# A hybrid decoder layer with 32 experts: expert weights loaded in transfers of two neighbouring units

## The reference

```python
x = x + jnp.einsum('bsd,de->bse', merged, w_out[l])
x = x + _moe(_rms_norm(x, g_ffn[l], RMS_EPS), w_router[l], b_router[l], w1[l], b1[l], w2[l], b2[l])
# in _moe: 32 experts, the top 4 of each token; for the tokens xb of an expert e:
gu = xb @ w1[e] + b1[e]                      # w1[e]: 1024 x 2048
gate, up = gu[:, :D_EXPERT], gu[:, D_EXPERT:]
gate = jnp.minimum(gate, SWIGLU_LIMIT)
up = jnp.clip(up, -SWIGLU_LIMIT, SWIGLU_LIMIT)
act = (up + 1.0) * (gate * jax.nn.sigmoid(SWIGLU_ALPHA * gate))
yb = act @ w2[e] + b2[e]                     # w2[e]: 1024 x 1024
```

## Time and profile before

| | us |
|---|---|
| median of 3 runs | 1905.17 (1902.64 to 1905.51) |
| profiled execution | 1906.27 |
| its span, first to last instruction | 1904.5 |
| mean granted TensorE clock | 0.993 of full speed |
| TensorE matmul busy | 1853.2 (97%) |
| VectorE busy | 1121.7 (59%) |
| ScalarE busy | 941.0 (49%) |
| GpSimd busy | 335.9 (18%) |
| DMA moved | 511.61 MB, mean 269 GB/s |

### The profile page before, as it was taken

How to read it: one execution, slowest core, us unless ns; L and a number is a source line. 1 busy time by engine, 2 the same in 40 slices (tenths; PEclk the granted TensorE clock), 3 DMA queues, 4 the chain that set the end, 5 groups by cost and what they waited for, 6 DMA issues and landing times.

```text
span 1904.5 us, 27272 instructions
## 1 busy us (share of the span) xinstructions
PE 1853.2 (97%) x8668; PEld 1311.0 (69%) x8668; DVE 1121.7 (59%) x1364; ACT 941.0 (49%) x1310; POOL 335.9 (18%) x401
## 2 busy tenths in 40 slices
PE   7999999999999999998999999999999999999998
PEld 5888888888888888886656655566556655665563
DVE  6767768768768433356745654455545654655466
ACT  4665765765667322234544444345435543445341
POOL 0321321322321000012111121112211220122010
PEclk8999999999999999998999999999999999999999
DMA  5231231331231332356899999999999999999998
GB/s 176 78 102 44 102 102 44 102 102 48 98 124 34 100 100 99 120 202 266 359 421 421 422 421 421 421 422 421 421 421 422 421 421 422 421 421 421 422 418 340
DMA packets 88286, 511.61 MB, mean 269 GB/s; under 512 B 12820, under 2 KB 15932, under 8 KB 37944
## 3 DMA queue, kind: packets, MB, share of 16 engines
q1 hardware_dynamic: 80728, 492.69, 64.7%
q0 software_dynamic: 6944, 16.36, 2.3%
q10 hardware_dynamic: 576, 2.10, 0.3%
HBM read 503.13 MB, written 25.44 MB: 278 GB/s over the span
## 4 chain that ended last, share of the span: by engine, by line
PE 73%; DMA 11%; DVE 9%; issue 4%; ACT 2%; SPq 0%; DVEq 0%; ACTq 0%
PE bank L1811 19%; PE bank L1238 15%; DMA big<-in_w 10%; PE bank L1620 10%; PE bank L1831 7%; PE bank L1840 6%; PE bank L1266 4%; PE bank L1823 2%; DVE w_lo L2370 2%; DVE wm_lo L948 1%; PE bank L1765 1%; DVE x_lo L2382 1%; PE bank L1387 1%; PE bank L1317 1%; DMA keep<-in_b 1%
## 5 line engine op out<-in xcount | busy, mean ns | idle before, releaser
L2370 DVE TENSOR_TENSOR w_lo<-big,w_hi 128x2048 fp32r<-128x2048 f32 x141 | 321.8, 2290 | 290.0 <-ACT w_hi L2078 289.9
L2078 ACT ACTIVATE w_hi<-big 128x2048 fp32r<-128x2048 f32 x141 | 268.8, 1918 | 319.6 <-DMA big<-in_w 305.6
L1831 PE MATMUL bank<-big,keep 128*64 128x512 f32 x896 | 203.1, 598 | 0.0
L1238 PE MATMUL bank<-h_hi,wm_hi 128*128 128x512 f32 x416 | 171.5, 412 | 2.6 <-ACT big L779 2.6
L1238 PE MATMUL bank<-h_hi,wm_lo 128*128 128x512 f32 x416 | 163.1, 392 | 0.0
L1238 PE MATMUL bank<-h_lo,wm_hi 128*128 128x512 f32 x416 | 162.4, 390 | 0.0
L2370 DVE TENSOR_TENSOR w_lo<-keep,w_hi 128x2048 fp32r<-128x2048 f32 x48 | 110.0, 2295 | 70.2 <-ACT w_hi L2078 70.2
L1811 PE MATMUL bank<-w_hi,x_hi 128*128 128x512 f32 x512 | 144.0, 403 | 5.6 <-DVE w_lo L2370 4.1
L1831 PEld LDWEIGHTS bank<-big,keep 128*64 128x64 f32 x896 | 60.0, 136 | 117.8 <-issue 117.8
L1811 PE MATMUL bank<-w_lo,x_hi 128*128 128x512 f32 x512 | 138.3, 392 | 0.0
L1811 PE MATMUL bank<-w_hi,x_lo 128*128 128x512 f32 x512 | 138.0, 391 | 0.0
(11 more groups left out here) (363 smaller groups left out, 3577.5 us busy)
## 6 DMA issues: line engine op xcount, KB each, us to landing
big<-in_w SPq DMA_DIRECT2D x288, 1024.0 KB, 13.3
keep<-in_w SPq DMA_DIRECT2D x96, 1024.0 KB, 13.2
big<-in_w_mix SPq DMA_DIRECT2D x72, 512.0 KB, 3.3
keep<-in_w_tail SPq DMA_DIRECT2D x44, 512.0 KB, 3.3
big<-y_tok SPq DMA_DIRECT2D x6, 1024.0 KB, 11.9
keep<-in_x SPq DMA_DIRECT2D x8, 512.0 KB, 5.3
big<-in_w_tail SPq DMA_DIRECT2D x4, 512.0 KB, 3.9
h_rows<-keep ACTq DMA_DIRECT2D x4, 512.0 KB, 4.4
```

Of the source, the lines that this page charges most:

```text
L1238: ins = pe.matmul(to[:], w[:, k], h[:, k], start=(k == 0 and w is hi and h is h_hi), stop=(k == KT - 1 and w is lo))
L1831: ins = pe.matmul(bank[2 * (c // 2)][r, :], x_s[:, n % 4, CS * (n // 4):CS * (n // 4 + 1)], raw[s][:, c * 512:(c + 1) * 512], start=False, ...
L2078: act.activation(w_hi[:, s], raw[r], ACT.Copy).then_inc(hi_ready, 1)
L2370: dve.tensor_tensor(w_lo[:, s], raw[r], w_hi[:, s].bitcast(F32), ALU.subtract).then_inc(lo_ready, 1)
```

## The change

1. `STEP` becomes 1 1 1 1 2 2 1 1 1 1 2 2: units (2, 0) and (2, 1) stand next to each other.
2. The eight raw places become four double ones: `raw_spots` is reordered so that places 2n and 2n+1 are neighbours in SBUF. `load_two` brings two units in one transfer of 2 MB, 128 partitions x 16 KB, after both places are free. Both units' consumers wait on the even place's semaphore (`landed_in`). `load` is kept for single units.
3. A partition's 16 KB are neighbouring rows: rows 2p and 2p+1 of 256 in w1, rows 4p to 4p+3 of 512 in w2. So the k parts are strided: `gate_rows` (every second column of the gathered tokens, which were contiguous) in the transposes of `turn_x_b` and `turn_x_s`, and `down_rows` every fourth instead of every second in those of the activations.
4. The first eight units are still single; units 7, 4, 5, 3, 6 come in this order, unit 3 after four uses of `w_out`.
5. The split of the unit at FIRST2 moves from the end of the step before to its place in the loop of step_s, behind `take_act_b`; in DVE's first step it stands ahead of `last_places`, that of (2, 1) behind it.
6. At the start of the experts VectorE does `w_lo` of unit 0 before it waits for the ranks, `w_lo` of unit 1 before the end of routing, `x_lo` next, then `row_half`, then `w_lo` of unit 2. TensorE's first product waits for `x_hi`, and for `x_lo` only ahead of the group that uses it.
7. In the mixer, PE waits for one `proj_read` less ahead of the first product of a head.

```diff
-STEP = ((1, 0), (1, 1), (1, 2), (1, 3), (2, 0), (1, 4), (1, 5), (2, 1), (1, 6), (1, 7), (2, 2), (2, 3))
+STEP = ((1, 0), (1, 1), (1, 2), (1, 3), (2, 0), (2, 1), (1, 4), (1, 5), (1, 6), (1, 7), (2, 2), (2, 3))
...
-    o = k // 2 * 2 * P + k % 2
-    return slice(o, o + 2 * P - 1, 2)
+    o = k // 4 * 4 * P + k % 4
+    return slice(o, o + 4 * P - 3, 4)
...
-        raw_spots = [(big, 3 * W), (big, 4 * W), (big, 5 * W), (big, 0), (big, W), (big, 2 * W), (keep, 21504), (keep, 19456)]
+        raw_spots = [(big, 4 * W), (big, 5 * W), (big, 2 * W), (big, 3 * W), (big, 0), (big, W), (keep, 19456), (keep, 21504)]
...
+                    elif use == 0:
+                        if not isinstance(j, int) or j > 0:
+                            pe.wait_ge(proj_read.sem, proj_read.at(j, 0) - 1)
...
-                for n in (3, 4, 5):
-                    sp.wait_ge(wout_used, n - 2)
-                    sp.dma_start(raw[n], w1[0, n]).then_inc(raw_in[n], 16)
+                for n, used in ((4, 1), (5, 2), (3, 4)):
+                    sp.wait_ge(wout_used, used)
+                    sp.dma_start(raw[n], gate_unit(slice(0, 1), n)).then_inc(raw_in[n], 16)
...
+                def load_two(j, kind, p, m, n, e):
+
+                    freed(j, kind, p + 1)
+                    s = slot_of(j, kind, p)
+                    assert s % 2 == 0 and n % 2 == 0 and slot_of(j, kind, p + 1) == s + 1
+                    w, k = (w1, 2) if m == 1 else (w2, 4)
+                    src = w[bass.ds(e, 1), k * n // 2:k * n // 2 + k].rearrange("a k p n -> (a k p) n").rearrange(
+                        "(p k) n -> p (k n)", k=k)
+                    sp.dma_start(raw_two[s // 2], src).then_inc(raw_in[s], 16)
...
                 def step(j, kind, e1, e2):
                     for p, (m, n) in enumerate(STEP):
-                        freed(j, kind, p)
-                        load(slot_of(j, kind, p), m, n, e1 if m == 1 else e2)
+                        if p % 2 == 0:
+                            load_two(j, kind, p, m, n, e1 if m == 1 else e2)
...
-                            c = (4 * half + k) * P
-                            ins = pe.transpose(bank[6 + half][:, k * CAP:(k + 1) * CAP], xg[:, c:c + P],
+                            ins = pe.transpose(bank[6 + half][:, k * CAP:(k + 1) * CAP], xg[:, gate_rows(4 * half + k)],
...
-                    for p in range(FIRST2 + 1, 12):
+                    for p in range(FIRST2, 12):
                         if STEP[p][0] == 2:
                             split(j, "S", p)
...
                     take_x_s(j + 1)
-                    split(j + 1, "S", FIRST2)
```

More of the change, by code:

```diff
@@ L450, in decoder_layer @@
         sg = aux[:, 2 * T:4 * T].rearrange("p (a n) -> p a n", a=2)
-        raw_spots = [(big, 3 * W), (big, 4 * W), (big, 5 * W), (big, 0), (big, W), (big, 2 * W), (keep, 21504), (keep, 19456)]
+        raw_spots = [(big, 4 * W), (big, 5 * W), (big, 2 * W), (big, 3 * W), (big, 0), (big, W), (keep, 19456), (keep, 21504)]
         raw = [t[:, at:at + W] for t, at in raw_spots]
+        raw_two = [t[:, at:at + 2 * W] for t, at in raw_spots[0::2]]
         first = [big[:, 6 * W + n * W:7 * W + n * W] for n in range(SPLIT)]
@@ L1418, in slot_of, with landed_in @@
                 return (KT + place_of(j, kind, p)) % RAW
+            def landed_in(j, kind, p):
+                s = slot_of(j, kind, p)
+                return raw_in[s if kind == "C" else s - s % 2]
             def landed(j, kind, p):
-                n = KT + place_of(j, kind, p)
-                return j * (24 // RAW) + (n // RAW + (0 if n % RAW < SPLIT else 1))
+                s, n = slot_of(j, kind, p), place_of(j, kind, p)
+                if kind == "C" and s % 2:
+                    return 1 + (1 if s >= SPLIT else 0)
+                return j * (24 // RAW) + (n // RAW + 1 + (1 if s - s % 2 >= SPLIT else 0))
             def landed_ov(o, i):
                 s = i % RAW_OV
-                return o * (12 // RAW_OV) + (UNITS // RAW + i // RAW_OV + (1 if s < SPLIT else 2))
+                before = (1 if s >= SPLIT else 0) + (1 if s % 2 else (NPAIR + 1) * (24 // RAW))
+                return o * (12 // RAW_OV) + (before + i // RAW_OV + 1)
             def pairs(eng, body, peel_first, peel_last):
@@ L1489, in _, with gate_unit @@
                 sp.dma_start(gffn_sb, gffn).then_inc(gffn_in.sem, 16)
+                def gate_unit(e, n):
+                    two = w1[e, n - n % 2:n - n % 2 + 2].rearrange("a k p n -> (a k p) n")
+                    return two.rearrange("(p k) n -> p k n", k=2)[:, n % 2]
                 for n in range(SPLIT):
-                    sp.dma_start(first[n], w1[0, n]).then_inc(first_in[n].sem, 16)
+                    sp.dma_start(first[n], gate_unit(slice(0, 1), n)).then_inc(first_in[n].sem, 16)
                 sp.wait_ge(y_filled, 16 * HEADS)
@@ L1565, in _ @@
                 e_prev, e_small = expert(2 * NPAIR), expert(2 * NPAIR + 1)
-                for p in range(12):
+                for p in range(0, 12, 2):
                     m, n = STEP[p]
[L1568 to L1572, removed]
+                    load_two(NPAIR, "S", p, m, n, e_small if m == 1 else e_prev)
+                for n in (0, 2):
+                    load_two(NPAIR, "B", n, 2, n, e_small)
                 sp.wait_ge(yout_b.sem, yout_b.at(NBIG - 1, 0))
@@ L1754, in turn_x_s @@
                     for k in range(4):
-                        ins = pe.transpose(bank[6][:, k * P:(k + 1) * P], xg_s[:, k * P:(k + 1) * P], ident)
+                        ins = pe.transpose(bank[6][:, k * P:(k + 1) * P], xg_s[:, gate_rows(k)], ident)
                     ins.then_inc(txs_ready.sem, 1)
@@ L1803, in bias2_s, with gate_up_b @@
                     pe.matmul(bank[4][:], pick_s[:], bias_hl[:, D:D + 512], start=True, stop=False)
-                def gate_up_b(u, s, n):
+                def gate_up_b(u, s, n, first=False):
                     pe.wait_ge(lo_ready, u + 1)
+                    if first and n % 4 == 0:
+                        pe.wait_ge(xh_ready.sem, xh_ready.at(0, n // 4 + 1))
                     hi, lo = x_hi[:, n], x_lo[:, n]
                     for x_part, w_part in ((hi, w_hi), (hi, w_lo), (lo, w_hi)):
+                        if first and n % 4 == 0 and x_part is lo:
+                            pe.wait_ge(xl_ready.sem, xl_ready.at(0, n // 4 + 1))
                         for c in range(4):
@@ L1853, in unit @@
                         s = slot_of(j, kind, p)
-                        pe.wait_ge(raw_in[s], landed(j, kind, p) * 16)
+                        pe.wait_ge(landed_in(j, kind, p), landed(j, kind, p) * 16)
                         (gate_up_s if m == 1 else down_s)(s, n)
@@ L1906, in down_last @@
                     s = slot_of(NPAIR, "B", n)
-                    pe.wait_ge(raw_in[s], landed(NPAIR, "B", n) * 16)
+                    pe.wait_ge(landed_in(NPAIR, "B", n), landed(NPAIR, "B", n) * 16)
                     down_s(s, n)
@@ L2071, in _, with split_at @@
                 ch.end()
-                def split_at(u, s, r, count):
-                    act.wait_ge(raw_in[r], count * 16)
+                def split_at(u, s, r, count, by=None):
+                    act.wait_ge(by or raw_in[r], count * 16)
                     if not isinstance(u, int) or u >= SPLIT:
@@ L2083, in split @@
                     assert of == "B"
-                    split_at(b_unit(j, i), (KT + i) % SPLIT, slot_of(j, kind, p), landed(j, kind, p))
+                    split_at(b_unit(j, i), (KT + i) % SPLIT, slot_of(j, kind, p), landed(j, kind, p),
+                             landed_in(j, kind, p))
                 def take_x_b(b):
@@ L2167, in _ @@
                 take_x_s(0)
-                split(0, "S", FIRST2)
                 pairs(act, body, True, False)
@@ L2358, in _, with first_low @@
                                   ALU.subtract).then_inc(wgt_ready, 1)
+                def first_low(n):
+                    dve.wait_ge(hi_ready, n + 1)
+                    dve.tensor_tensor(w_lo[:, n], first[n], w_hi[:, n].bitcast(F32), ALU.subtract).then_inc(lo_ready, 1)
+                first_low(0)
                 dve.wait_ge(rank_ready.sem, rank_ready.at(1))
@@ L2361, in _ @@
                 dve.tensor_copy(rank, bank[4][:, 128:128 + E])
-                for n, (to, of) in enumerate(SMALL_ROWS):
-                    ins = dve.tensor_scalar(row_half[to], rows[of, 0:E], 2.0, float(n // 2), ALU.mult, ALU.add)
-                ins.then_inc(halves_ready, 1)
+                first_low(1)
                 ch.end()
@@ L2445, in step_s @@
                     for p in range(FIRST2, 12):
-                        if STEP[p][0] == 2 and p > FIRST2:
+                        if STEP[p][0] == 2:
                             split(j, "S", p)
@@ L2505, in last_places @@
                     ch.end()
[L2507 to L2511, removed]
+                take_x_b(0)
+                for n, (to, of) in enumerate(SMALL_ROWS):
```

(3 more changed lines are left out.)

24 lines of the change are left out of this document (10 added, 14 removed).

## The result

The changed kernel takes **1911.07 us** (median of 20 runs, 1901.94 to 1921.27), the kernel before 1905.29 (20 runs, 1902.64 to 1907.44): ratio 1.0032, interval 1.0022 to 1.0043. I had forecast 1890.6, and not more than 1905. The runs also spread over 19 us, where those of before spread over 5. The profiled execution took 1919.69 us, its span 1917.8, near the slow end; so the sizes that I take from it are too large for the median.

A forecast was written before the change was run, and what follows sets the result against it. DMA was taken to bound the expert loop, 62.3 us a turn (24 MB) against TensorE's 60.3. Transfers -13.0, mixer -2.6, first turn +0.5, last turn +0.5 make -14.6 us: 1890.6 against the median, range 1883 to 1905.

The forecast's parts named there:

- The transfers: Expert loop: fewer, larger packets save 0.9 us a turn, giving turns of 61.4 us; 13.0 us over 14.5 turns.
- The double places: Expert loop: S8, S9 are issued in time by 0.6 us, so the DMA gap is taken as 0.
- rival D: Expert loop: S0 and S1's place frees so late that the queue runs dry before S8 every turn; slower, 1919.6; chance 0.12.
- The first turn: Start of experts: S5's split behind last_places stalls TensorE 4.1 us, but the 18th unit lands only 0.5 us later (0 to 3).
- The mixer: Mixer: waiting for one read less at each head's first product saves 2.6 us (bounds 0 and 2.6).
- 0.6 us to spare is less than the gathers shift a landing: Reason for the rival that double places make a gap up to 1 us a turn: 1893 to 1905, chance 0.17.

The follow-up runs named there:

- e6: The changed kernel with last_places moved behind the split of the second down unit: 1905.59 us, ratio 1.0003 to the kernel before.
- e9: e6 with the second half of turn_x_b's token transposes done three times (8 more a turn): 1894.24 us, ratio 0.9939 to the kernel before.
- e1: The changed kernel with each unit in its own 1 MB transfer, issued when its own place is free and waited for alone: 1903.78 us, ratio 0.9994 to before.
- e7: e1 with last_places moved behind the split of the second down unit: 1900.90 us, ratio 0.9976 to the kernel before.
- e2: e1 with both loads of a pair issued only when both places are free: 1907.00 us, ratio 1.0012 to the kernel before.
- e8: e1 with both units of a pair having to land before the first is used: 1908.60 us, ratio 1.0014 to the kernel before.
- e3: e2 with both units of a pair also having to land before the first is used: 1916.67 us, ratio 1.0065 to the kernel before.

## Why the prediction was wrong

**The transfers: right.** 0.9 us a turn, turns of 61.4: e6 shows 61.50, 0.8 us less than before, and 427 GB/s as long as nothing disturbs it.

**The double places: the step that failed.** I laid the order on the unstalled turn, found 0.6 us to spare at the pair S8, S9 and took the gap as 0. For undisturbed turns the gap is 0 indeed. But I had put the 1 us that TensorE then waits ahead of S10 at nothing, since DMA is the bound, and that is the term that failed. The wait is 1.5 us undisturbed and 2.2 on average in the changed kernel. Ahead of S10 no fall of the clock followed a wait of 1.6 us or less (e6, e9); after many of 1.7 to 3.3 us one did. I had counted the clock only once, at the start, at 0 to 3 us.

How the 14 turns from 974.72 us on add up can be read from the trace. Each is 60.1 us of TensorE's own work, plus its wait ahead of S10, plus 1.5 if the clock falls. The six turns with a fall took 63.5 to 64.9 us, five behind one and without one 62.2 to 62.9, the three others 61.3 to 61.9. The falls are 9 us in all and the waits 30.8, where turns of 61.4 would have left 19 for them. So of the 21 us over my forecast some 9 are the falls themselves and 12 the longer waits. The medians point the same way: of the 20 runs of the changed kernel, the fastest (1901.94) has the highest mean clock, 0.995, and the two slowest (1919.69 and 1921.27) have 0.985 and 0.987.

A late turn delays the next, as release and landing are coarse. Which pair it shows at was another than I had picked. One's issue to landing at 1170.1 us (S8 and S9) and at 1213.3 (S0 and S1 of the next turn, whose places are free after B5), both in the turn with a fall from 1166.38 on:

```profile
DMA to landing us min/median/max: 10.2/10.2/10.2
...
DMA to landing us min/median/max: 7.8/7.8/7.8
```

In an undisturbed turn of e6 they are 9.7 and 9.4 us. So the queue runs near dry ahead of the next S0 and not before S8, and then the pair S10, S11 of that next turn takes 12.46 us for 11.67 in the chain above. It is rival D in kind (a double place comes free so late that the queue runs dry), but not in its place, nor in its trigger: D should have needed a gap in every turn from the places alone.

The cause is shown in two halves. Without falls (e9) the pairs gain, and with falls but without pairs (e1, e7) nothing is lost. e2, e8 and e3 (3.2, 4.2, 12.9 us) don't give the price of the places alone, as their traces have three, four and seven falls. What is argued only is the last link, why the next S10 lands later when the queue ran near dry 40 us ahead of it.

**The first turn: mis-sized.** The stall I had at 4.1 us, measured 3.67. For the whole I had +0.5 (0 to 3), since DMA is the bound; moving last_places is worth 5.4 us. The stall lowers the clock, and DMA is not full behind it: 402 GB/s and not 421 up to 1034 us. I had followed DMA's issues only to the 18th unit and taken the rest as full. Of the 5.4 us, 3.5 don't hang on pairs, as e7 against e1 shows.

**The mixer: mis-sized the other way,** 4.7 us, where I had 2.6 as the most.

**The sum, in the profiled execution.** Before, L1765 ahead of the first S0 stood at 912.16; it is at 906.74, -5.4 (I had -4.0). First turn +5.9. The 14 turns from 974.72 to 1855.38 take 880.7 us, for 869.9: +10.8, where I had -13. From there to the end 62.4 for 60.4: +2.0. Together +13.3, the difference of the spans. The median of 20 runs is 5.8 above.

**Range and chances.** I had left out a loss of this kind at 0.12 and cut the range at 1905. The sentence "for it: 0.6 us to spare is less than the gathers shift a landing" was a reason to widen, and I did not follow it. The rule of the Trainium skill ("DMA: Bandwidth & Descriptors", section Bandwidth) to batch transfers to at least 1 MiB is met by both kernels; larger ones still gained, 6.3 us in all. The 2.0 us a transfer stand on the same page of the Trainium skill, in section "Anatomy of one DMA — SWDGE (gpsimd) path", as a fit for transfers that GpSimd issues. They aren't what is won here: 12 transfers fewer brought 0.8 us a turn, since transfers overlap.

## What to carry to other kernels

Joining two transfers makes the bytes cheaper and the buffers coarser: a place is freed when the last half is used, and the first half can be used only when the last has landed. Where the queue is the bound and the consumer nearly so, count what both have to spare, in sum, before you take the cheaper bytes. A wait of TensorE that "costs nothing" because something else is the bound isn't free if the clock falls after it and the buffers are too coarse to make up for it: look at the length of the single wait, not at its share, and if need be give TensorE work there. Here last_places at a later place took the loss from 5.8 us to 0.4, and 8 transposes a turn turned that into a gain of 11.0, of which the mixer's wait is 4.7.

## What the runs showed of the hardware

- Loads of 2 MB in packets of 16 KB halve the packets and make a byte cheaper by 2% against 1 MB in packets of 8 KB, 37.7 for 38.4 us of engine time per MB (e6 and before); the core moved 427 GB/s for 421.
- The DMA share doesn't tell a near-dry queue: the changed kernel's is 1.00 at 417 GB/s, e6's 1.01 at 427. Slow packets count as busy: from 1100 to 1600 us 154 packets of 16 KB in the changed kernel took over 1 us, for a median of 0.61, and in e6 23 did; of the 16 in the turn from 1166.38 on, 13 start within 2.2 us of the issue at 1213.3. Issue to landing (7.7 against 9.1 us at the least) tells it.
- Waits of TensorE of about 2 us, once in 62, were followed by 1.2 GHz in some turns and not in others. The times of the changed kernel are uneven, 19 us between its 20 runs (5 between the 20 of before, 1.7 between the four of e9), and go with the mean clock; e1, with such waits but single transfers, spreads over 6.5.
